# Three norm seams of a two-layer prefix model: the first tile's split, and when four weight splits are made

## The chip, the cores and the metric

The kernel runs on one NeuronCore of a Trainium2 chip. The metric is the device time of one execution in microseconds (us). Five engines have a part: TensorE (PE, with its weight loads as PEld), VectorE (DVE), ScalarE (ACT), GpSimd (POOL), and SyncE (SP), which issues the DMAs. They run side by side and wait for each other on semaphores.

## The reference, cut to what matters

Two layers work on 256 tokens of `x` and 256 of `ctx`. Each layer is a mixer (HGRN2 in layer 0, Mamba2 in layer 1) and a convolutional feed-forward net (FFN). Around each of these stands the same pattern:

```python
x = x + mx[2] * rmsnorm(yx, post_norm[l, 0])            # gate, norm and add what the mixer gave
hx = modulate(rmsnorm(x, pre_norm[l, 1]), mx[3], mx[4]) # norm again: h * (1 + scale) + shift
yx = conv_ffn(hx, ffn_w_up[l], ffn_w_down[l], ...)      # the next products read hx
```

All is float32. `rmsnorm` needs the mean square over all 1024 channels of a token.

## The kernel before, in words

Activations lie with channels on partitions: 8 tiles (KT = 8) of 128 channels x 512 tokens (256 where only `x` is left, in layer 1 from the mixer's end on). TensorE multiplies them in a split form: every operand is a rounded high part plus a low part, and a product is three matmuls, high*high, high*low, low*high. For activations these parts are `hh` and `hl`, for weights `wh` and `wl`. A weight block of 1024 columns per partition (8 k-tiles of 128x128) lands by DMA in one of four slots of `wraw`; ScalarE writes its high part (`split_hi`), VectorE (`split_lo`), or GpSimd in a loop of the FFN, its low part. VectorE's splits are counted by one semaphore, `w_lo_dve`, in the order of the blocks.

The order of each engine's work is written out by hand. Three times between two stages there is a *seam*, where `add_and_norm(l, s, n, weights)` runs on VectorE: seam 0 ahead of the first FFN (n = 512), seam 1 ahead of the Mamba projections (n = 512), seam 2 ahead of the second FFN (n = 256). Ahead of it VectorE makes `products` of each of the 8 output tiles (with ScalarE's squares), TensorE adds them up over the channels with a matrix of ones (`both_sums`), ScalarE makes a reciprocal root, and `variance` gives the second norm's mean square from the sums. TensorE then does one or two blocks of the modulation product (`ada_block`).

In `add_and_norm` VectorE runs over the tiles m: it "turns" tile m (`turn`: `sq <- yT * bank`, the first norm), adds it to `xT` (two instructions for the two halves of 256 tokens), turns tile m+1, and writes the second norm `tmp <- xT * bank`. ScalarE's `shift_high` scales and shifts `tmp` in place (two instructions) and copies it, rounded, to `hh`. GpSimd's `norm_low` writes `hl = tmp - hh`. After tile 0 VectorE does the splits of the blocks named in `weights`.

TensorE goes on with `by_tile`: a batch of three or four projections, k-tile by k-tile, so that it can start as soon as the first tile is there. Ahead of the batch it waits by `need_sub` for the last of the batch's weight blocks (in the FFN of both layers the fourth one, `u0 + 3`; at seam 1 block `("b", 0)`), and then for `hl_ready` of tile 0:

```python
need_sub(u0 + 2)
need_sub(u0 + 3)
by_tile(hl_count - KT, [up(0, 0), up(0, 1), up(1, 0), up(1, 1)], n)
```

Of the kernel before, what the change touches and what calls it, by code (L numbers as in the profile page):

```python
# [12 lines left out]
F32 = mybir.dt.float32  # L13
F32R = mybir.dt.float32r
U32 = mybir.dt.uint32
ALU = mybir.AluOpType
ACT = mybir.ActivationFunctionType
# [123 lines left out]
def program(nc, a, out):  # L141
# [542 lines left out]
    def _(pool):  # L684
# [81 lines left out]
        def norm_low(i, n):  # L766

            hh0 = (2, 3, 5)[i] * KT
            for k in range(KT):
                pool.wait_ge(hh_ready, hh0 + k + 1)  # L770
                pool.tensor_tensor(hl[:, k, 0:n], tmp[:, k % 2, 0:n], hh[:, k, 0:n].bitcast(F32), ALU.subtract).then_inc(hl_ready, 1)  # L771

# [37 lines left out]
    def _(act):  # L810
# [52 lines left out]
        def shift_high(i, l, s, n=T):  # L863

            for m in range(KT):
                if m < KT - 1:
                    hf[0] += 1
                    act.wait_ge(hf_ready, hf[0])
                else:
                    plan.wait_emptied(act, ("r2", i // 2, i % 2))  # L870
                t = tmp[:, m % 2, :]
                for b in range(n // SEQ):
                    r = slice(b * SEQ, (b + 1) * SEQ)
                    ins = act.activation(t[:, r], t[:, r], ACT.Identity, scale=nsc[:, l, s, m, b:b + 1],
                                         bias=mod[:, l, 3 * s * KT + m, b:b + 1])
                step(ins)
                step.wait()
                act.activation(hh[:, m, 0:n], t[:, 0:n], ACT.Copy).then_inc(hh_ready, 1)  # L878
# [451 lines left out]
    def _(dve):  # L1330
# [3 lines left out]
        def split_lo(n, i=0, lo=0, hi=None):  # L1334

            size = subs[n][0]
            hi = size if hi is None else hi
            if lo == 0:
                dve.wait_ge(w_hi, i * 4 + (n + 1))
            s = n % SLOTS  # L1340
            ins = dve.tensor_tensor(wl[:, s, lo:hi], wraw[:, s, lo:hi], wh[:, s, lo:hi].bitcast(F32), ALU.subtract)  # L1341
            if hi == size:
                ins.then_inc(w_lo["dve"], 1)
# [87 lines left out]
        def add_and_norm(l, s, n, weights):  # L1431

            i = 2 * l + s
            first, second = ("r", l, s), ("r2", l, s)
            turned = {}
            rn[0] += 1

            def turn(m):

                ins = V.tensor_tensor(sq[:, m % 2, 0:n], yT[:, m, 0:n], bank[plan.bank(first)][:, 0:n], ALU.mult)  # L1440
                if m < KT - 1:
                    turned[m] = step(ins)
                else:
                    plan.empty(ins, "dve", first)

            dve.wait_ge(rb_ready, i + 1)
            turn(0)
            for m in range(KT):
                if m < KT - 1:
                    step.wait(turned[m])  # L1450
                else:
                    plan.wait_emptied(dve, first)
                for b in range(n // SEQ):
                    r = slice(b * SEQ, (b + 1) * SEQ)
                    ins = V.scalar_tensor_tensor(out=xT[:, m, r], in0=sq[:, m % 2, r], scalar=gsc[:, l, s, m, b:b + 1],
                                                 in1=xT[:, m, r], op0=ALU.mult, op1=ALU.add)
                ins.then_inc(x_new, 1)
                xn[0] += 1
                if m < KT - 1:
                    turn(m + 1)  # L1460
                if m == 0:
                    dve.wait_ge(rstd_ready, rn[0])
                if m >= 2:
                    dve.wait_ge(hl_ready, KT * (i + 1) + m - 1)
                dve.wait_ge(x_new, xn[0])
                if (l, s, m) == (0, 1, 0):
                    plan.wait_ready(dve, ("am", LATE + 6))
                ins = V.tensor_tensor(tmp[:, m % 2, 0:n], xT[:, m, 0:n], bank[plan.bank(second)][:, 0:n], ALU.mult)
                if m < KT - 1:
                    ins.then_inc(hf_ready, 1)  # L1470
                else:
                    plan.empty(ins, "dve", second)
                if m == 0:
                    for w in weights:
                        split_lo(w)
            hhn[0] += KT

        xn, rn, norms = [0], [0], [0]
# [266 lines left out]
        gate_scales(0, 1)  # L1745
        step.wait()
        u0 = at["up", 0, 0, 0, 0]
        for m, pieces in enumerate(((at["y", 0, 5],), (at["y", 0, 6],), (at["y", 0, 7],), (), (u0,), (u0 + 1,), (u0 + 2,), ())):
            plan.wait_emptied(dve, ("y", 0, m))
            products(0, 0, 0, m, T)  # L1750
            for w in pieces:
                split_lo(w)
            if m == 3:
                ada_add(LATE + 2)
        variance(0, 0, T)
        add_and_norm(0, 0, T, (u0 + 3,))

        def taps(l, n):

# [101 lines left out]
        psum_freed_dve = plan.freed["dve"]  # L1861
        ffn_dve(0, T, True)
        variance(0, 1, T)
        add_and_norm(0, 1, T, (at["b", 0] - 1, at["b", 0]))

        u, e, w = dtw[:, 0, :], dtw[:, 1, :], dtw[:, 2, :]

# [242 lines left out]
            if m == 4:  # L2110
                ada_add(LATE + 10)
        variance(1, 0, SEQ)
        add_and_norm(1, 0, SEQ, [at["up", 1, 0, 1, j] for j in range(2)])
        ffn_dve(1, SEQ, False)
        dve.wait_ge(rstd_ready, rn[0] + 1)
        plan.wait_emptied(dve, ("xr", 1, 1))
# [637 lines left out]
```

## Time and profile before

| | |
|---|---|
| median of three runs | 1396.06 us (1392.92, 1396.06, 1396.13) |
| the profiled execution | 1392.95 us, its span 1391.2 us |
| TensorE busy | 1325.3 us, 95% of the span |
| VectorE, ScalarE, GpSimd busy | 894.1, 648.1, 331.6 us |
| mean granted TensorE clock | 0.986 of full speed |
| seam 0, seam 1, seam 2 | around 431, 812 and 1176 us |

TensorE is busy nearly all the time, and 82% of the chain of work that ended last is its matmuls. What is left are single stretches in which it waits. The profiled execution lies 3.1 us below the median of the three runs.

### The profile page before, as it was taken

The page shows a single profiled execution, that of the slowest core. Times are in us where ns is not written, and L with a number is a line of the kernel's source. Part 1 is how long each engine was busy: PE and PEld are TensorE (multiplying, and loading weights), DVE is VectorE, ACT ScalarE, POOL GpSimd, SP SyncE. Part 2 cuts the span into 40 slices and gives each one's busy share as a digit, 9 for nine tenths or more (in the row PEclk, how much of TensorE's full clock was granted, in tenths as well). Part 3 has the DMA queues.
Part 4 walks back from the last instruction along what each step waited for, and adds up shares of the span by engine and source line. Part 5 has one row for each costly group of instructions (what it writes and reads, how often), then busy time and mean ns, then how long its engine had stood idle before and what let it go on. Part 6 is the DMA issues. An engine that isn't in the chain of part 4 may idle for free.

```text
span 1391.2 us, 21288 instructions
## 1 busy us (share of the span) xinstructions
PE 1325.3 (95%) x7893; PEld 1118.1 (80%) x7893; DVE 894.1 (64%) x1706; ACT 648.1 (47%) x1023; POOL 331.6 (24%) x227
## 2 busy tenths in 40 slices
PE   5999999999998999999999989999999988899997
PEld 2678888888675888888888757888888877899997
DVE  4567777677587644322455778777777857665573
ACT  4435445444346433223333266555555645654554
POOL 1000000000202654105551030211111301780961
PEclk9999999999999999999999999999999999999999
DMA  9643343335461632333324424433333465456743
GB/s 346 180 133 125 122 129 127 125 90 184 152 202 41 181 91 76 91 106 109 102 68 136 116 96 122 152 92 91 91 91 91 137 207 157 124 164 176 203 134 107
DMA packets 274788, 183.16 MB, mean 132 GB/s; under 512 B 6643, under 2 KB 249107, under 8 KB 274707
## 3 DMA queue, kind: packets, MB, share of 16 engines
q1 hardware_dynamic: 274162, 180.00, 42.8%
q10 hardware_dynamic: 544, 2.10, 0.4%
q8 instruction: 49, 0.80, 0.2%
q14 instruction: 33, 0.26, 0.1%
HBM read 181.03 MB, written 1.05 MB: 131 GB/s over the span
## 4 chain that ended last, share of the span: by engine, by line
PE 82%; DVE 10%; ACT 5%; issue 2%; DMA 1%; POOL 0%; DVEq 0%; ACTq 0%
PE bank L2135 20%; PE bank L2137 20%; PE bank L2136 20%; DVE wl L1341 3%; PE bank L2150 2%; PE bank L2151 2%; PE bank L2152 2%; ACT wh L820 1%; PE bank L2201 1%; PE bank L2250 1%; DVE conv L1800 1%; PE bank L2682 1%; PE bank L2709 1%; PE bank L2277 1%; PE bank L2696 1%
## 5 line engine op out<-in xcount | busy, mean ns | idle before, releaser
L2135 PE MATMUL bank<-hh,wh 128*128 128x512 f32 (+1 forms) x1298 | 460.6, 355 | 10.2 <-DVE wl L1341 4.5
L2137 PE MATMUL bank<-hh,wl 128*128 128x512 f32 (+1 forms) x1298 | 455.8, 351 | 0.0
L2136 PE MATMUL bank<-hl,wh 128*128 128x512 f32 (+1 forms) x1298 | 455.6, 351 | 0.0
L820 ACT ACTIVATE wh<-wraw 128x1024 fp32r<-128x1024 f32 (+2 forms) x265 | 256.4, 985 | 108.9 <-PE bank L2137 97.4
L1341 DVE TENSOR_TENSOR wl<-wraw,wh 128x1024 fp32r<-128x1024 f32 (+2 forms) x187 | 205.8, 1122 | 136.6 <-ACT wh L820 136.5
L2135 PEld LDWEIGHTS bank<-hh,wh 128*128 128x128 f32 x1298 | 247.1, 190 | 45.0 <-DVE wl L1341 7.0
L2137 PEld LDWEIGHTS bank<-hh,wl 128*128 128x128 f32 x1298 | 247.1, 190 | 32.5
L2136 PEld LDWEIGHTS bank<-hl,wh 128*128 128x128 f32 x1298 | 247.2, 190 | 30.4
L1800 DVE SCALAR_TENSOR_TENSOR conv<-bank,pv,conv 128x189 f32<-128x189 f32 (+3 forms) x396 | 173.1, 437 | 131.9 <-ACT conv L1093 103.6
L711 POOL TENSOR_TENSOR wl<-wraw,wh 128x1024 fp32r<-128x1024 f32 x78 | 187.0, 2406 | 175.0 <-ACT wh L820 174.6
L2135 PE MATMUL bank<-fh,wh 128*128 128x512 f32 (+1 forms) x352 | 120.0, 341 | 3.5 <-DVE wl L1341 3.1
L2136 PE MATMUL bank<-fl,wh 128*128 128x512 f32 (+1 forms) x352 | 119.0, 338 | 0.0
L2137 PE MATMUL bank<-fh,wl 128*128 128x512 f32 (+1 forms) x352 | 119.0, 338 | 0.0
L756 POOL TENSOR_TENSOR hl<-yT,hh 128x512 fp32r<-128x512 f32 x13 | 19.0, 1487 | 369.7 <-DVE gates L1697 357.7
L2135 PEld LDWEIGHTS bank<-fh,wh 128*128 128x128 f32 x352 | 66.2, 188 | 12.1 <-issue 1.7
L771 POOL TENSOR_TENSOR hl<-tmp,hh 128x512 fp32r<-128x512 f32 (+1 forms) x24 | 27.9, 1164 | 196.1 <-ACT hh L878 196.1
L2137 PEld LDWEIGHTS bank<-fh,wl 128*128 128x128 f32 x352 | 66.2, 188 | 8.0
L2136 PEld LDWEIGHTS bank<-fl,wh 128*128 128x128 f32 x352 | 66.2, 188 | 7.9
L797 POOL TENSOR_TENSOR wx<-xtok,wtk 128x512 f32<-128x512 f32 x16 | 16.9, 1056 | 221.9 <-ACT xtok L1226 162.1
L1093 ACT ACTIVATE conv<-bank,pv 128x512 f32<-128x512 f32 (+1 forms) x44 | 29.4, 667 | 72.8 <-PE bank L2137 72.8
L731 POOL TENSOR_TENSOR fl<-prod,fh 128x512 f32 (+3 forms) x44 | 49.9, 1134 | 55.1 <-ACT fh L1109 55.1
L2150 PE MATMUL bank<-hh,wh 128*128 128x512 f32 (+2 forms) x119 | 47.5, 400 | 15.7 <-POOL hl L771 15.3
(338 smaller groups left out, 1936.2 us busy)
## 6 DMA issues: line engine op xcount, KB each, us to landing
wraw<-in_ffn_w_up SPq DMA_DIRECT2D x88, 512.0 KB, 3.9
araw<-in_ada_w SPq DMA_DIRECT2D x40, 1024.0 KB, 7.2
wraw<-in_mb_w_in SPq DMA_DIRECT2D x48, 512.0 KB, 4.1
wraw<-in_hg_w_in SPq DMA_DIRECT2D x40, 512.0 KB, 3.8
wraw<-in_ffn_w_down SPq DMA_DIRECT2D x32, 512.0 KB, 3.8
wraw<-in_mb_w_out SPq DMA_DIRECT2D x16, 512.0 KB, 4.4
gates<-in_ada_w SPq DMA_DIRECT2D x5, 1024.0 KB, 9.3
wraw<-in_hg_w_out SPq DMA_DIRECT2D x8, 512.0 KB, 4.8
```

The costliest lines, as they stand in the source:

```text
L711: pool.tensor_tensor(wl[:, n % SLOTS, 0:size], wraw[:, n % SLOTS, 0:size], wh[:, n % SLOTS, 0:size].bitcast(F32), ALU.subtract).then_inc(w ...
L731: pool.tensor_tensor(fl[:, bass.ds(i * 2 + c, 1), 0:w], prod[:, c % 2, 0:w].unsqueeze(1), fh[:, bass.ds(i * 2 + c, 1), 0:w].bitcast(F32), ...
L771: pool.tensor_tensor(hl[:, k, 0:n], tmp[:, k % 2, 0:n], hh[:, k, 0:n].bitcast(F32), ALU.subtract).then_inc(hl_ready, 1)
L820: act.activation(wh[:, n % SLOTS, 0:size], wraw[:, n % SLOTS, 0:size], ACT.Copy).then_inc(w_hi, 1)
L1093: act.activation(conv[:, u, 0:n], bank[2 * u if src is None else src][:, 0:n], ACT.Identity, scale=pv[:, bass.ds(i * 2 + (cw + c), 1)], bi ...
L1341: ins = dve.tensor_tensor(wl[:, s, lo:hi], wraw[:, s, lo:hi], wh[:, s, lo:hi].bitcast(F32), ALU.subtract)
L1800: ins = V.scalar_tensor_tensor(out=o(conv[:, u, :]), in0=src(bank[up]), scalar=pv[:, bass.ds(i * 2 + (cw + row * FT + c), 1)], in1=o(conv[ ...
L2135: pe.matmul(dst, W, hi(k), start=(k == 0), stop=False, **skip)
L2136: pe.matmul(dst, W, lo(k), start=False, stop=False, **skip)
L2137: ins = pe.matmul(dst, L, hi(k), start=False, stop=(k == nk - 1), **skip)
L2150: pe.matmul(dst, W, hi(k), start=(k == 0), stop=False, skip_group_check=True)
L2151: pe.matmul(dst, W, lo(k), start=False, stop=False, skip_group_check=True)
```

## The change

The matrix work and its order on TensorE stay as they are. On the other engines:

- ScalarE writes the shifted tile 0 straight into `hh[:, 0]` (rounded on the way), without the step over `tmp` and the copy.
- VectorE makes tile 0's low part itself: it shifts `tmp` a second time into `rsq` and subtracts `hh`. GpSimd begins with tile 1.
- In `add_and_norm` the norm of tile 0 comes ahead of the turn of tile 1.
- Weight splits: at seam 0 the splits of `u0 + 1` and `u0 + 2` move from behind the products of tiles 5 and 6 to behind those of tile 7. The splits inside `add_and_norm` move: at seam 0 the one from behind tile 0 to behind tile 1, at seam 1 the two from behind tile 0 to behind tiles 1 and 2, at seam 2 the second from behind tile 0 to behind tile 1.

```diff
@@ norm_low (GpSimd)
-            for k in range(KT):
+            pool.wait_ge(hl_ready, KT * (i + 1) + 1)
+            for k in range(1, KT):
@@ shift_high (ScalarE)
-                    ins = act.activation(t[:, r], t[:, r], ACT.Identity, scale=nsc[:, l, s, m, b:b + 1],
-                                         bias=mod[:, l, 3 * s * KT + m, b:b + 1])
+                    ins = act.activation(hh[:, 0, r] if m == 0 else t[:, r], t[:, r], ACT.Identity,
+                                         scale=nsc[:, l, s, m, b:b + 1], bias=mod[:, l, 3 * s * KT + m, b:b + 1])
+                if m == 0:
+                    ins.then_inc(hh_ready, 1)
+                    continue
@@ add_and_norm (VectorE)
-                if m < KT - 1:
+                if 0 < m < KT - 1:
                     turn(m + 1)
...
                 if m == 0:
-                    for w in weights:
-                        split_lo(w)
+                    turn(1)
+                    dve.wait_ge(hf_ready, KT + (KT - 1) * i + 1)
+                    for b in range(n // SEQ):
+                        r = slice(b * SEQ, (b + 1) * SEQ)
+                        ins = V.tensor_scalar(rsq[:, r], tmp[:, 0, r], nsc[:, l1, s1, 0, b:b + 1],
+                                              mod[:, l1, 3 * s1 * KT, b:b + 1], ALU.mult, ALU.add)
+                    step(ins)
+                    dve.wait_ge(hh_ready, hhn[0] + 1)
+                    step.wait()
+                    V.tensor_tensor(hl[:, 0, 0:n], rsq[:, 0:n], hh[:, 0, 0:n].bitcast(F32), ALU.subtract).then_inc(hl_ready, 1)
+                if m < 3 and weights[m] is not None:
+                    split_lo(weights[m])
@@ seam 0
-        for m, pieces in enumerate(((at["y", 0, 5],), (at["y", 0, 6],), (at["y", 0, 7],), (), (u0,), (u0 + 1,), (u0 + 2,), ())):
+        for m, pieces in enumerate(((at["y", 0, 5],), (at["y", 0, 6],), (at["y", 0, 7],), (), (u0,), (), (), (u0 + 1, u0 + 2))):
...
-        add_and_norm(0, 0, T, (u0 + 3,))
+        add_and_norm(0, 0, T, (None, u0 + 3, None))
@@ seam 1
-        add_and_norm(0, 1, T, (at["b", 0] - 1, at["b", 0]))
+        add_and_norm(0, 1, T, (None, at["b", 0] - 1, at["b", 0]))
@@ seam 2
-        add_and_norm(1, 0, SEQ, [at["up", 1, 0, 1, j] for j in range(2)])
+        add_and_norm(1, 0, SEQ, [at["up", 1, 0, 1, j] for j in range(2)] + [None])
```

VectorE's order at the end of seam 0's products, before (`gates` holds the running sums, `sq` the squares, `wl <-wraw,wh` is a weight split):

```order
L1410 TENSOR_TENSOR sq<-sq 128x512
L1341 TENSOR_TENSOR wl<-wraw,wh 128x1024
L1384 SCALAR_TENSOR_TENSOR gates<-yT,gsc,xT 128x256 x2
L1399 SCALAR_TENSOR_TENSOR gates<-sq,gsq,gates 128x256 x2
L1406 TENSOR_TENSOR gates<-gates 128x512
L1410 TENSOR_TENSOR sq<-sq 128x512
L1341 TENSOR_TENSOR wl<-wraw,wh 128x1024
L1384 SCALAR_TENSOR_TENSOR gates<-yT,gsc,xT 128x256 x2
L1399 SCALAR_TENSOR_TENSOR gates<-sq,gsq,gates 128x256 x2
L1418 TENSOR_TENSOR sq<-bank,rstd 128x512
```

and now:

```order
L1414 TENSOR_TENSOR sq<-sq 128x512
L1388 SCALAR_TENSOR_TENSOR gates<-yT,gsc,xT 128x256 x2
L1403 SCALAR_TENSOR_TENSOR gates<-sq,gsq,gates 128x256 x2
L1410 TENSOR_TENSOR gates<-gates 128x512
L1414 TENSOR_TENSOR sq<-sq 128x512
L1388 SCALAR_TENSOR_TENSOR gates<-yT,gsc,xT 128x256 x2
L1403 SCALAR_TENSOR_TENSOR gates<-sq,gsq,gates 128x256 x2
L1345 TENSOR_TENSOR wl<-wraw,wh 128x1024 x2
L1422 TENSOR_TENSOR sq<-bank,rstd 128x512
```

Both splits now stand behind the last tile's products, directly ahead of the variance.

VectorE's order in `add_and_norm` of seam 1, before (`tmp<-xT,bank` is the second norm of a tile):

```order
L1440 TENSOR_TENSOR sq<-yT,bank 128x512
L1455 SCALAR_TENSOR_TENSOR xT<-sq,gsc,xT 128x256 x2
L1440 TENSOR_TENSOR sq<-yT,bank 128x512
L1468 TENSOR_TENSOR tmp<-xT,bank 128x512
L1341 TENSOR_TENSOR wl<-wraw,wh 128x1024 x2
L1455 SCALAR_TENSOR_TENSOR xT<-sq,gsc,xT 128x256 x2
L1440 TENSOR_TENSOR sq<-yT,bank 128x512
L1468 TENSOR_TENSOR tmp<-xT,bank 128x512
```

and now, from the norm of tile 0 to the second split:

```order
L1473 TENSOR_TENSOR tmp<-xT,bank 128x512
L1445 TENSOR_TENSOR sq<-yT,bank 128x512
L1483 TENSOR_SCALAR rsq<-tmp,nsc,mod 128x256 x2
L1488 TENSOR_TENSOR hl<-rsq,hh 128x512
L1460 SCALAR_TENSOR_TENSOR xT<-sq,gsc,xT 128x256 x2
L1445 TENSOR_TENSOR sq<-yT,bank 128x512
L1473 TENSOR_TENSOR tmp<-xT,bank 128x512
L1345 TENSOR_TENSOR wl<-wraw,wh 128x1024
L1460 SCALAR_TENSOR_TENSOR xT<-sq,gsc,xT 128x256 x2
L1445 TENSOR_TENSOR sq<-yT,bank 128x512
L1473 TENSOR_TENSOR tmp<-xT,bank 128x512
L1345 TENSOR_TENSOR wl<-wraw,wh 128x1024
```

The second split stood five instructions behind the first turn; it now ends this row of twelve, behind the norms of tiles 1 and 2. At seams 0 and 2 the last split stands where the first one stands here, behind the norm of tile 1.

TensorE's rows where the batch of seam 0 begins, with the semaphores that they wait for (in the changed kernel; before they are the same but for line numbers):

```order
L2216 MATMUL bank<-gates,scc 32x512 x3
L2216 MATMUL bank<-alate,scc 32x512 [waits a_landed2]
L2216 MATMUL bank<-alate,scc 32x512 x3
L2165 MATMUL bank<-hh,wh 128x512 [waits hl_ready,w_lo_dve]
L2166 MATMUL bank<-hl,wh 128x512
L2167 MATMUL bank<-hh,wl 128x512
```

The first matmul of the batch waits for two things, tile 0's low part and VectorE's weight splits; nothing moved here.

## Rows read from the trace of the kernel before

**Rows 1.** Who TensorE waited for, whole span: total us, times, longest us.
```profile
PE bank L2150 <- POOL hl L771: 15.3, 4, 5.2
PE bank L2135 <- DVE wl L1341: 7.5, 7, 1.6
```

**Rows 2.** The chain of waits at seam 0: start us, us, what.
```profile
426.91 0.46 issue
427.37 0.69 DVE tmp L1468
428.08 1.10 ACT tmp L874 x2
429.20 0.64 ACT hh L878
429.91 1.27 POOL hl L771
431.32 0.77 PE bank L2150
```

**Rows 3.** Timeline of seam 0, VectorE: start us, us, instruction, idle before it.
```profile
418.00 1.22 DVE L1341 TENSOR_TENSOR wl<-wraw,wh 128x1024 fp32r<-128x1024 f32 x1
...
422.01 0.69 DVE L1418 TENSOR_TENSOR sq<-bank,rstd 128x512 f32<-128x512 f32 x1 [1.21 <-PE bank L2447]
...
426.77 0.68 DVE L1440 TENSOR_TENSOR sq<-yT,bank 128x512 f32<-128x512 f32 x1
...
427.96 1.22 DVE L1341 TENSOR_TENSOR wl<-wraw,wh 128x1024 fp32r<-128x1024 f32 x1
429.10 0.87 DVE L1455 SCALAR_TENSOR_TENSOR xT<-sq,gsc,xT 128x256 f32<-128x256 f32 x2
429.89 0.68 DVE L1440 TENSOR_TENSOR sq<-yT,bank 128x512 f32<-128x512 f32 x1
430.49 0.68 DVE L1468 TENSOR_TENSOR tmp<-xT,bank 128x512 f32<-128x512 f32 x1
```

**Rows 4.** Timeline of seam 0, TensorE's first sum of the squares.
```profile
418.23 1.10 PE L2445 MATMUL bank<-sq,ones 128*128 128x512 f32 x2 [2.57 <-DVE sq L1410]
```

**Rows 5.** Timeline of the first norm, VectorE: the shift and the low part.
```profile
33.13 0.73 DVE L1496 TENSOR_SCALAR tmp<-tmp,nsc,mod 128x256 f32<-128x256 f32 x2
33.78 0.69 DVE L1502 TENSOR_TENSOR hl<-tmp,hh 128x512 fp32r<-128x512 f32 x1
```

**Rows 6.** Timeline of seam 1: VectorE, GpSimd, TensorE.
```profile
808.16 0.68 DVE L1468 TENSOR_TENSOR tmp<-xT,bank 128x512 f32<-128x512 f32 x1
808.76 2.35 DVE L1341 TENSOR_TENSOR wl<-wraw,wh 128x1024 fp32r<-128x1024 f32 x2
811.03 1.88 DVE L1455 SCALAR_TENSOR_TENSOR xT<-sq,gsc,xT 128x256 f32<-128x256 f32 x2
...
810.71 1.52 POOL L771 TENSOR_TENSOR hl<-tmp,hh 128x512 fp32r<-128x512 f32 x1 [62.99 <-ACT hh L878]
...
812.38 0.77 PE L2150 MATMUL bank<-hh,wh 128*128 128x512 f32 x1 [5.25 <-POOL hl L771]
...
817.32 0.50 PE L2150 MATMUL bank<-hh,wh 128*128 128x512 f32 x1 [0.36 <-POOL hl L771]
```

**Rows 7.** Timeline of seam 2: VectorE, TensorE.
```profile
1172.83 0.42 DVE L1468 TENSOR_TENSOR tmp<-xT,bank 128x256 f32<-128x256 f32 x1 [0.16 <-ACT bank L861]
...
1176.25 0.55 PE L2150 MATMUL bank<-hh,wh 128*128 128x256 f32 x1 [4.73 <-POOL hl L771]
...
1179.15 0.58 PE L2150 MATMUL bank<-hh,wh 128*128 128x256 f32 x1
```

**Rows 8.** Windows of 7 us from each batch's start: us, PE busy, PEclk, DMA.
```profile
431.32:438.32 7.00, 7.00 (x19) 0.60 0.17 50
812.38:819.38 7.00, 6.63 (x21) 0.76 0.41 122
1176.25:1183.25 7.00, 6.99 (x39) 0.66 0.45 131
```

More of the change, by code:

```diff
@@ L1433, in add_and_norm @@
             i = 2 * l + s
+            l1, s1 = (i + 1) // 2, (i + 1) % 2
             first, second = ("r", l, s), ("r2", l, s)
```

## The prediction

> **What bounds the kernel now.** I read the page first: TensorE is busy for 95% of the span, so time is won or lost only where it waits. Then the list of who TensorE waited for [rows 1]: the largest entry is the first product of a batch waiting for a low part from GpSimd, 15.3 us in 4 waits, the three long ones at the three seams (about 5 us each [rows 6, 7]). Then the chain of waits at seam 0 [rows 2]: VectorE's norm of tile 0, ScalarE's shift (1.10) and copy (0.64), GpSimd's subtraction (1.27), and TensorE starts at 431.32. Last the timelines around the seams [rows 3 to 7] and the granted clock behind each start [rows 8]. The reader is to see there that the chain is what ended last *before*, and that a second condition, VectorE's last weight split, was met only shortly ahead of it: at 429.18 against 431.2 at seam 0 (427.96 + 1.22 [rows 3]), and at 811.11 against 812.23 at seam 1 (808.76 + 2.35 and 810.71 + 1.52 [rows 6]). TensorE's order, shown with the change, has both waits on the batch's first matmul. The change shortens the chain and moves the last split to behind the norm of tile 1 or 2. So the question at each seam is when that split ends.
>
> **The steps on VectorE.** Where instructions follow without a wait, the next starts about 0.08 before the last one's recorded end. From start to start, for 512 columns: a turn 0.60, the two adds to `xT` 0.79, a norm 0.60, a split 1.14 [rows 3]; the two shifts 0.65 [rows 5]. The low part takes 0.69 and frees VectorE after about 0.62 [rows 5].
>
> **What is won ahead of the first norm.** *Norm before turn.* The norm of tile 0 stood at 427.37, behind a turn begun at 426.77; in the chain that is 0.46 of "issue" [rows 2, 3]. Without the turn the norm starts once the adds have landed, 0.44 earlier. At seam 2 it is not the turn but ScalarE that it waits for (0.16 idle, released by ScalarE [rows 7]): nothing there. *Two splits behind the last products* (seam 0 only). TensorE's first sum waits 2.57 us for VectorE's sum of squares of tile 6 [rows 4], and one split stands ahead of that, so the sums come 1.1 earlier. The two splits then run behind tile 7's products, which end 2.2 earlier than before; they end when the sums are there, so the variance starts at 420.9 in place of 422.01 [rows 3]. Won: 1.1. In bounds from nothing (the splits push the variance back) to 1.2 (its idle time).
>
> **From the first norm to the last split.** Counted from the start of tile 0's norm: the turn of tile 1 begins at +0.60, the shifts at +1.20, done at about +1.9. ScalarE's two halves take +0.71 to +1.81 [rows 2]; a write rounded on the way is not in the trace with these operands; the copy of the same width costs 0.64 against 1.10 for the two halves, so I leave the 1.10 and bound an extra by 0 to 0.2. The low part starts at +1.9 and is there at +2.6, where it was at 431.18 - 427.37 = +3.8 before: 1.2 won on this leg. But VectorE is busy with it. Adds at +2.55, turn +3.35, norm of tile 1 +3.95, split +4.55 to +5.77, and TensorE starts 0.05 later. At seam 1 the adds, turn and norm of tile 2 follow (5.69 + 0.79 + 0.60 + 0.60), and the last split runs from +7.68 to +8.9.
>
> **Seam 0.** The norm starts at 427.37 - 1.1 - 0.44 = 425.83. Low part there at 428.4, but the split ends at 431.6, and TensorE starts at 431.65 against 431.32: **+0.35**. All that was won ahead is used up by the split's new place.
>
> **Seam 1.** The norm starts at 808.16 - 0.44 = 807.72, the last split ends at 816.6, TensorE starts at 816.7 against 812.38 [rows 6]: +4.3. Before, it had a second wait of 0.36 at 817.32 for tile 1; now tile 1 is ready (norm at 811.67, plus the 3.8 of the old chain is 815.5), so -0.36. After the first k-tile TensorE sets the pace itself, so nothing of the lost start comes back. Two smaller terms. The granted clock: in the 7 us behind the start it is 0.60, 0.76 and 0.66 [rows 8]; full speed being 2.4 GHz and the lower level 1.2, that is 5.6, 3.4 and 4.8 us at the lower one, and half of each is lost: 2.8, 1.7, 2.4. Seam 1, the cheapest, would now follow 9.6 us of idle time in place of 5.25. I put it near the mean of all, +0.6, in bounds of -1.7 to +1.1; the other two I leave, each within 1 either way. GpSimd: adds that began beside its subtraction took 1.88 in place of 0.87 [rows 3, 6]. The last split now begins at 815.4 while GpSimd works on tile 1 (814.3 to 815.6): +0.2, in bounds of 0 to 1.0. In sum **+4.7**.
>
> The Trainium skill (TensorE: Matmul & The Clock Gate, "What's actually happening") says that how many matmuls run at the half clock after a pause changes from run to run. The trace agrees in that the three seams differ, 3.4 to 5.6 us, after pauses alike. By that rule the clock term has no sign, and the sum would be 5.8 in place of 6.4.
>
> **Seam 2.** 256 columns. The norm stays at 1172.83. ScalarE's single piece (about 0.6 after the norm's end) is done at 1173.9, and the low part at 1174.4. VectorE: split to 1175.4, adds, turn and norm of tile 1 (0.40, 0.34, 0.34, as the 0.42 of [rows 7] less the overlap), second split 1176.5 to 1177.7. TensorE starts at 1177.8 against 1176.25: +1.55; the second k-tile, which came 2.90 after the first where 12 products at the lower clock need about 2.6 to 2.7, no longer waits: -0.2. **+1.35**.
>
> **Nothing elsewhere.** GpSimd loses three subtractions and is idle for tens of us ahead of them [rows 6]. The loads that reuse the slots of the late splits start up to 5 us later, but their blocks are wanted only behind the batch, over 15 us on. The norms of tiles 2 to 7 come 0.4 later at seam 0, some 4 us later at seam 1; TensorE, at 12 products per tile, stays behind them.
>
> **Sum.** 0.35 + 4.7 + 1.35 = 6.4 us, so the profiled execution of 1392.95 would become 1399.35. That execution lies 3.1 under the median of the three runs, 1396.06; against the median it is **1402.4**, of which the uncertain places take -2.5 to +3.
>
> **The rivals.**
> *The chain alone sets the start (faster).* If the last split did not hold the batch, TensorE would start with the low part: at seam 0 at 428.55 (-2.8; tile 2 at 436.7 gives back 0.4), at seam 1 at 810.45, bounded by tile 1 at 815.5 in place of 817.26 (-1.8), at seam 2 some -0.7. Together -4.9: 1391.2. For it speaks that GpSimd's chain is the wait that the profile names at all three seams; against it, that the batch's first matmul also waits for `w_lo_dve` and that the split's place is known to the instruction. 6%.
> *The late start is bought back (no change).* Behind each batch TensorE waits for a split again, 7.5 us in 7 waits over the kernel [rows 1]. Would these shrink by their mean of 1.1 behind each of the three batches, 3.2 us would be left: 1399.3. Against it: these splits wait for a slot that the batch's own last tile frees, so they move with it. Together with a lucky clock at the seams, 16%.
> *The dearer case (slower).* The pause at seam 1 makes the lower clock last as long as at seam 0 and longer, and the two-input work of VectorE and GpSimd collide at the split and at the adds behind it: +1.1 + 1.0 + 1.0 on the forecast, 1405.5. 12%.
>
> The Trainium skill (GPSIMD Engine Reference, "1. Specifications") says that GpSimd shares its way into SBUF with VectorE, and that they hinder each other where VectorE has two SBUF inputs, as its splits have. The 1.88 against 0.87 agrees; by that rule the last split at seam 1 would wait for GpSimd's end and start at about 815.6, the 0.2 taken above.
>
> **How the numbers follow.** The forecast, +6.4, has 66%, with a range of its own of 1399 to 1405.5. A change under 0.3% (4.2 us) can't be told from none. Slower: nine tenths of the forecast's 66 and the 12, 71%. No change: the 16, the rest of the forecast, and a part of the first rival, 25%. Faster: 4%. The range that should hold 8 in 10: 1396.5 to 1406.5; it takes in most of the case that buys time back and leaves out the faster one.
>
> **What would show it right or wrong.** In the profile of the changed kernel the first product of the batch should be released by VectorE's split `wl` and no more by a low part, at all three seams, with 5.5 to 6.5 us of idle time at seams 0 and 2 and about 9.5 at seam 1. The low part of tile 0, now VectorE's, should be there some 3 us ahead of it at seam 0 and 6 at seam 1. The variance of seam 0 should start about 1.1 earlier. Wrong would be a start of the batch right behind the low part, a batch at seam 1 that ends less than 3 us later against its seam's first norm than before, or a total under 1398.

## The result, and the profile after

| | before | changed |
|---|---|---|
| median of six runs each, us | 1392.76 (1390.88 to 1396.13) | 1400.13 (1397.81 to 1400.79) |
| span of the profiled execution, us | 1391.2 | 1398.7 |
| mean granted TensorE clock | 0.986 | 0.982 |

The changed kernel takes 1.0048 times as long, with a 95% interval of 1.0036 to 1.0060: slower, by about what was forecast (1402.4 against 1396.06, 1.0046). The profiled executions differ by 7.5 us.

Whom TensorE waited for, changed kernel, whole span (total us, times, longest us); this answers to [rows 1].

```profile
PE bank L2165 <- DVE wl L1345: 22.6, 3, 9.7
PE bank L2150 <- DVE wl L1345: 7.6, 7, 1.6
```

The wait for GpSimd's low part is gone from this list; in its place the batch waits three times for a weight split (`wl`), and longer. VectorE at seam 0, changed kernel (start us, us, instruction, idle before it), against [rows 3]:

```profile
423.94 0.43 DVE L1433 TENSOR_SCALAR ssx<-ssx 128x512 f32<-128x512 f32 x1
...
425.98 0.69 DVE L1473 TENSOR_TENSOR tmp<-xT,bank 128x512 f32<-128x512 f32 x1
426.59 0.68 DVE L1445 TENSOR_TENSOR sq<-yT,bank 128x512 f32<-128x512 f32 x1
427.19 0.73 DVE L1483 TENSOR_SCALAR rsq<-tmp,nsc,mod 128x256 f32<-128x256 f32 x2
428.02 0.69 DVE L1488 TENSOR_TENSOR hl<-rsq,hh 128x512 fp32r<-128x512 f32 x1
428.63 0.88 DVE L1460 SCALAR_TENSOR_TENSOR xT<-sq,gsc,xT 128x256 f32<-128x256 f32 x2
429.42 0.68 DVE L1445 TENSOR_TENSOR sq<-yT,bank 128x512 f32<-128x512 f32 x1
430.02 0.68 DVE L1473 TENSOR_TENSOR tmp<-xT,bank 128x512 f32<-128x512 f32 x1
430.62 1.22 DVE L1345 TENSOR_TENSOR wl<-wraw,wh 128x1024 fp32r<-128x1024 f32 x1
```

The norm of tile 0 starts 1.39 earlier than before (425.98 for 427.37), and its low part is there at 428.71. TensorE starts only at 431.93, 0.09 behind the end of the split at 431.84. Seam 1, VectorE and GpSimd, against [rows 6]:

```profile
808.51 0.69 DVE L1473 TENSOR_TENSOR tmp<-xT,bank 128x512 f32<-128x512 f32 x1
...
810.54 0.69 DVE L1488 TENSOR_TENSOR hl<-rsq,hh 128x512 fp32r<-128x512 f32 x1
...
813.14 1.22 DVE L1345 TENSOR_TENSOR wl<-wraw,wh 128x1024 fp32r<-128x1024 f32 x1
...
816.26 1.24 DVE L1345 TENSOR_TENSOR wl<-wraw,wh 128x1024 fp32r<-128x1024 f32 x1
...
815.15 1.27 POOL L772 TENSOR_TENSOR hl<-tmp,hh 128x512 fp32r<-128x512 f32 x1 [66.68 <-ACT hh L882]
```

TensorE where the three batches start, changed kernel; the last row is the next wait behind the batch of seam 1:

```profile
431.93 0.76 PE L2165 MATMUL bank<-hh,wh 128*128 128x512 f32 x1 [6.58 <-DVE wl L1345]
817.56 0.80 PE L2165 MATMUL bank<-hh,wh 128*128 128x512 f32 x1 [9.66 <-DVE wl L1345]
1184.66 0.55 PE L2165 MATMUL bank<-hh,wh 128*128 128x256 f32 x1 [6.34 <-DVE wl L1345]
...
843.69 0.39 PE L2150 MATMUL bank<-hh,wh 128*128 128x256 f32 x1 [0.64 <-DVE wl L1345]
```

and that last row in the kernel before:

```profile
837.96 0.39 PE L2135 MATMUL bank<-hh,wh 128*128 128x256 f32 x1 [0.64 <-DVE wl L1341]
```

At seam 1 the low part of tile 0 is done at 811.23, 6.3 us ahead of its first use. No second wait is left in that batch. Windows of 7 us from each start (us, busy times, then PEclk, DMA share, GB/s), against [rows 8]:

```profile
431.93:438.93 7.00, 7.00 (x19) 5.53 (x20) 7.00 (x13) 4.05 (x8) 3.82 (x3) 0.58 0.27 77
817.56:824.56 7.00, 7.00 (x19) 5.07 (x20) 7.00 (x13) 4.03 (x8) 3.78 (x3) 0.57 0.28 76
1184.66:1191.66 7.00, 7.00 (x43) 7.00 (x44) 6.70 (x16) 4.69 (x10) 4.00 (x5) 0.71 0.40 115
```

At seam 1 the clock is 0.57 where it was 0.76: the cheap seam has become as dear as seam 0.

**Where the 7.5 us are.** How far the changed execution lags at each landmark: 0.1 ahead of seam 0, 0.8 ahead of seam 1 (seam 0 itself cost 0.7), 5.7 behind seam 1's batch (5.0), 6.8 ahead of seam 2 (1.1), 7.9 behind it (1.1), 7.5 at the end. The 1.1 between seams 1 and 2 is one wait, in the Mamba layer, at a place where no instruction was moved. VectorE there, first the kernel before, then the changed one with GpSimd and TensorE beside it:

```profile
1108.58 0.73 DVE L1969 COPY_PREDICATED wd<-past,wd 128x512 f32<-128x512 uint32 x1
```

```profile
1114.32 1.85 DVE L1984 COPY_PREDICATED wd<-past,wd 128x512 f32<-128x512 uint32 x1
1111.47 5.79 POOL L756 TENSOR_TENSOR hl<-yT,hh 128x512 fp32r<-128x512 f32 x4
1116.89 0.63 PE L2228 MATMUL bank<-ident,asum 128*128 128x128 f32 x4 [1.09 <-DVE wd L1976]
```

GpSimd in the kernel before, at the same moment:

```profile
1108.58 1.83 POOL L756 TENSOR_TENSOR hl<-yT,hh 128x512 fp32r<-128x512 f32 x1
```

In both traces a subtraction of GpSimd begins together with the copy. Before, the copy kept its 0.73 and the subtraction took 1.83; in the changed kernel the copy took 1.85, and the subtraction beside it 1.26. One of the two loses time to the other, and TensorE waits only where it is VectorE. In the profiles of all ten experiments below the copy lost (1.85 or 1.86) and the wait of 1.1 is there, and one of them (e5) has no instruction of the change, only matmuls of constants in the pauses. So no part of the change is needed for it; the profile of before is the one without it. What decides which of the two loses was not tried.

### The profile page after: what moved, and what is told of

Its sections match the earlier page's. It is cut to its first block, busy times and chain, and to the rows that moved or that the text cites. A ratio compares the mean times of both kernels' runs of the same rounds, so it can differ in the third digit from the quotient of the medians.

```text
span 1398.7 us, 21296 instructions
## 1 busy us (share of the span) xinstructions
PE 1326.2 (95%) x7893; PEld 1118.4 (80%) x7893; DVE 893.9 (64%) x1714; ACT 646.1 (46%) x1020; POOL 327.6 (23%) x224
## 3 DMA queue, kind: packets, MB, share of 16 engines
HBM read 181.03 MB, written 1.05 MB: 130 GB/s over the span
## 4 chain that ended last, share of the span: by engine, by line
PE 81%; DVE 11%; ACT 4%; issue 1%; DMA 1%; SPq 1%; POOL 0%; DVEq 0%; ACTq 0%
PE bank L2150 20%; PE bank L2152 20%; PE bank L2151 20%; DVE wl L1345 3%; PE bank L2165 2%; PE bank L2216 2%; PE bank L2166 2%; PE bank L2167 2%; DMA gates<-in_ada_w 1%; ACT wh L821 1%; PE bank L2265 1%; DVE conv L1815 1%; PE bank L2724 1%; PE bank L2292 1%; PE bank L2711 1%
## 5 line engine op out<-in xcount | busy, mean ns | idle before, releaser
L772 POOL TENSOR_TENSOR hl<-tmp,hh 128x512 fp32r<-128x512 f32 (+1 forms) x21 | 23.6, 1123 | 199.9 <-ACT hh L882 199.9
```

## The experiments

Each kernel was run against the kernel before on the same chip. For the seams one measure is used throughout: the time from the start of `variance`'s last instruction on VectorE (`ssx`, 423.94 above) to the first row behind the batch in which TensorE waits (843.69 above). "Start" is the time to the batch's first matmul. The ratios rest on 5 to 12 runs of each kernel, the two columns on the right on one profiled execution each.

| kernel | ratio to before (95%) | start, seams 0 / 1 / 2 | to the batch's end, seams 0 / 1 / 2 |
|---|---|---|---|
| before | 1 | 6.4 / 6.7 / 5.0 | 31.5 / 32.3 / 20.5 |
| changed | 1.0048 (1.0036, 1.0060) | 8.0 / 11.1 / 6.7 | 33.2 / 37.2 / 21.6 |
| e1 own block | 1.0005 (0.9995, 1.0015) | 4.8 / 5.0 / 3.3 | 30.2 / 34.0 / 21.4 |
| e2 splits back | 1.0004 (0.9995, 1.0013) | 6.0 / 7.1 / 5.6 | 31.3 / 33.2 / 20.9 |
| e3 only splits | 1.0034 (1.0021, 1.0047) | 7.5 / 11.5 / 5.5 | 32.6 / 37.3 / 20.8 |
| e4 changed, pauses filled | 1.0007 (0.9998, 1.0016) | 8.0 / 11.1 / 6.7 | 30.5 / 34.5 / 20.0 |
| e5 before, pauses filled | 0.9988 (0.9978, 0.9998) | 6.4 / 6.7 / 5.1 | 29.3 / 33.8 / 19.7 |
| e7 own block, filled | 1.0008 (0.9999, 1.0017) | 4.8 / 5.0 / 3.3 | 31.4 / 34.0 / 20.9 |
| e8 own block, early supply | 0.9983 (0.9974, 0.9992) | 4.8 / 5.0 / 3.3 | 31.3 / 32.1 / 20.6 |
| e6 e8, filled | 0.9983 (0.9974, 0.9992) | 4.8 / 5.0 / 3.3 | 31.3 / 32.1 / 20.8 |
| e9 before, one split early, filled | 0.9953 (0.9939, 0.9967) | 6.4 / 6.4 / 5.1 | 29.3 / 30.1 / 19.7 |
| e10 e9, norms first, filled | 0.9969 (0.9955, 0.9983) | 6.1 / 6.1 / 5.3 | 30.0 / 30.8 / 19.8 |

**e1: each product waits for its own block.** The changed kernel, with the wait for the batch's last block replaced by one wait per product at its first k-tile.

```diff
-                    need_sub(u0 + 2)
-                    need_sub(u0 + 3)
-                    by_tile(hl_count - KT, [up(0, 0), up(0, 1), up(1, 0), up(1, 1)], n)
+                    by_tile(hl_count - KT, [up(0, 0), up(0, 1), up(1, 0), up(1, 1)], n, own=[u0 + j for j in range(4)])
@@ by_tile; likewise at seam 1
-                for dst, w, nk, finish in products:
+                for j, (dst, w, nk, finish) in enumerate(products):
+                    if own is not None and k == 0:
+                        need_sub(own[j])
```

> The changed kernel; only TensorE's waits differ: each product of the batch waits for its own weight block at the first k-tile, where all four used to be waited for ahead of the first matmul. Theory A (the last split holds the batch's start): the batch starts with VectorE's low part of tile 0, about 3.1 us earlier than in the changed kernel at seam 0 (428.8), 6.1 at seam 1 (811.4) and 3.3 at seam 2. The last block is wanted only after nine matmuls, so seam 0 no longer waits for it, seams 1 and 2 wait a little inside the first k-tile. The end of the batches moves by -2.9, -4.2 and -1.8 us (less what the clock takes): about -9 against the changed kernel, -1.5 to -2.5 against the one before (1390 to 1391). Theory B (VectorE's added work on tile 0 is what costs, the splits do not): no gain beyond 1 us, 1399 to 1400.

Median 1394.04; the span is 7.7 shorter than the changed kernel's. TensorE's waits in the batches of this kernel, seams 0 to 2:

```profile
PE bank L2167 <- DVE hl L1488: 10.0, 3, 3.6
PE bank L2167 <- DVE wl L1345: 4.0, 4, 1.8
PE bank L2167 <- POOL hl L772: 0.4, 1, 0.4
```

The starts are now released by VectorE's low part (`hl`) and come 3.2, 6.1 and 3.4 sooner. So the split's gate on the first matmul is what the change paid for. But the batch only reaches the splits later: at seam 1 it waits 0.46 and 1.76 for them, and ends 1.7 later than before. Starting early on the low part wins at seam 0 alone. That is less than expected (1390 to 1391): against the changed kernel the batches end 3.1, 3.2 and 0.2 sooner, where I had 2.9, 4.2 and 1.8.

**e2: the splits of `add_and_norm` back.** The changed kernel, with both splits right behind tile 0's low part.

```diff
-                if m < 3 and weights[m] is not None:
-                    split_lo(weights[m])
+                if m == 0:
+                    for w in weights:
+                        if w is not None:
+                            split_lo(w)
```

> The changed kernel with the splits of add_and_norm back behind tile 0, now right behind its low part; the two splits behind the last products stay. Theory A: the last split ends about +3.85 us behind the norm of tile 0 at seam 0 (it was +5.85), +5.0 at seam 1 (+9.0) and +3.85 at seam 2 (+5.0). TensorE starts 2.0, 4.0 and 1.1 us earlier than in the changed kernel: -7.1 in sum, 1393, no difference from before that can be measured. Theory B: VectorE's added work is still there, so no more than 1 us is won against the changed kernel.

Median 1393.8, as expected: the loss is gone although VectorE still makes tile 0's low part. The split still releases all three starts, after 4.6, 5.7 and 5.3 us.

**e3: only the splits move.** The kernel before with the splits at their new places (two at seam 0 ahead of the variance, four inside `add_and_norm`) and nothing else.

```diff
                 if m == 0:
-                    for w in weights:
-                        split_lo(w)
+                if m < 3 and weights[m] is not None:
+                    split_lo(weights[m])
@@ seam 0, 1, 2
+        pieces (), (), (u0 + 1, u0 + 2) behind tiles 5, 6, 7
+        weights (None, u0 + 3, None); (None, at["b", 0] - 1, at["b", 0]); [..., None]
```

> The kernel before with only the moves of the splits (two behind the last products at seam 0; behind tiles 1 and 2 in place of tile 0). Low part of tile 0 by GpSimd as before. Theory A: the last split ends +3.75 us behind the norm of tile 0 at seam 0, level with the low part, so only the 1.1 of the products is won; at seam 1 the split ends at about 815.1, TensorE starts +2.8 against before; at seam 2 +0.35. With 0.7 of clock at seam 1: +2.5 against before, 1395.3. The rest of the change's +7 (some 4.5) is then what VectorE's new work in front of the split costs. Theory B: the moves alone cost nothing, 1391 to 1392.

Measured +5.0 us (1398.18 for 1393.17), twice what I expected. VectorE, GpSimd and TensorE at seam 1 of this kernel:

```profile
811.96 2.89 DVE L1455 SCALAR_TENSOR_TENSOR xT<-sq,gsc,xT 128x256 f32<-128x256 f32 x2
...
810.78 3.78 POOL L771 TENSOR_TENSOR hl<-tmp,hh 128x512 fp32r<-128x512 f32 x2 [63.00 <-ACT hh L878]
...
817.23 0.80 PE L2149 MATMUL bank<-hh,wh 128*128 128x512 f32 x1 [10.03 <-DVE wl L1341]
```

GpSimd's subtractions of tiles 0 and 1 now lie beside the first split (810.82 to 812.04) and the adds of tile 2. The split keeps its 1.22 and the subtraction beside it takes 2.38; the adds take 2.89 in place of 0.87, and the two subtractions together 3.78 in place of 2 x 1.27. The last split moves back by those 2 us as well. At seam 0 it is the slowed subtraction itself that the batch waits for (7.5 for 6.4). So the moved splits alone cost 5 of the 7.4 us. With the low part on VectorE too, the batches end 0.6 later, 0.1 sooner and 0.8 later, and the intervals of the two kernels overlap. That it costs so little fits the traces, in which the changed kernel has no subtraction of tile 0 on GpSimd to collide with; this was not tried apart. The two halves don't add up, and my division of the loss between them was wrong.

**e4: the pauses filled, changed kernel.** TensorE multiplies constants (24, 36 and 24 matmuls of 128x128 into a bank that is overwritten later) in the three pauses. They leave the supply as it is and keep the engine at work.

```diff
+        def keep_busy(count):
+            for _ in range(count):
+                pe.matmul(bank[3][:, 0:P], ones[:, :], ident[:, :], start=True, stop=True)
@@ ahead of each of the three batches
+        keep_busy(24)      # 36 at seam 1, 24 at seam 2
```

> The changed kernel; TensorE fills the pause of each seam with small matmuls of constants into a bank that is overwritten later (24, 36 and 24 of 128x128, some 5.2, 7.8 and 5.2 us), and waits then as before. If the low clock behind each batch's start (5.9, 6.0 and 4.1 us of the first 7 in the changed kernel) comes from the pause and not from the batch itself, the granted clock stays at 1.0 and half of that time is won back: 2.9 + 3.0 + 2.0 = -8 against the changed kernel, 1392. If the clock falls all the same, no difference; if the fill delays the batch, the start is released by nothing on VectorE and comes later than 431.9.

Median 1393.75, 6.4 under the changed kernel where I had expected 8. The fill at seam 1 (36 matmuls, each recorded as two), the batch's start behind it, and the window from there:

```profile
805.16 8.30 PE L2174 MATMUL bank<-ident,ones 128*128 128x128 f32 x72
814.90 0.50 PE L2165 MATMUL bank<-hh,wh 128*128 128x512 f32 x1 [1.44 <-DVE wl L1345]
```

```profile
814.90:821.90 7.00, 7.00 (x31) 5.27 (x32) 7.00 (x13) 4.01 (x7) 3.80 (x3) 1.00 0.29 78
```

The batches start as late as in the changed kernel (same "start" column) and run at full clock: they end 2.8, 2.7 and 1.6 sooner. That is the price of the lower clock at the seams, measured apart from the waiting: 7.1 us in all, where the windows above give 2.9, 3.0 and 2.0 (half of the time at the lower level). The median spans agree with it, 1391.4 for 1398.4. The times gain less because in six of e4's eleven executions the time lies 2.4 to 3.5 over the span, where it is 1.7 to 1.9 in every other kernel; why is open.

**e5: the pauses filled, kernel before** (19, 20 and 18 of the same matmuls).

> The kernel before; TensorE fills the three pauses (5.0, 5.25 and 4.7 us) with 19, 20 and 18 small matmuls of constants, about 0.23 us each by the last runs. Theory C (the low clock behind a seam is paid only where TensorE, not the supply of tiles, sets the pace): seam 0 wins until tile 1 holds it, -1.9; seam 1 nothing, since its second k-tile already waited for tile 1 and ran at full clock from there; seam 2 -0.9. Sum -2.8 against before. Theory D (every us at the low clock costs half a us): 2.8 + 1.7 + 2.4 = -6.9.

Median 1391.29: only 1.5 us won where the three seams could have given 6.9 by [rows 8] (2.8, 1.7 and 2.4) and the other of my two recorded sums was 2.8. Seams 0 and 2 ended 2.2 and 0.8 sooner. Seam 1 got worse, 33.8 in place of 32.3, in a profiled execution (1393.75) that lies 2.5 above the median. The second wait in its batch, and the window behind it:

```profile
815.33 0.50 PE L2150 MATMUL bank<-hh,wh 128*128 128x512 f32 x1 [1.90 <-POOL hl L771]
```

```profile
817.43:824.43 7.00, 7.00 (x28) 5.30 (x27) 7.00 (x13) 5.13 (x10) 2.96 (x3) 0.86 0.01 2
```

At full clock the first k-tile is used up sooner, tile 1 isn't there, the wait grows from 0.36 [rows 6] to 1.90, and behind it the clock falls after all. Not every such wait has this sequel: at seam 2 of the same profile the batch waits 1.23 for tile 1, and the 7 us behind it ran at 1.00.

**e7: own block and fill together** (e1 with 12, 12 and 10 matmuls), **e8: own block with an earlier supply** (e1, and `norm` of tile 1 ahead of turn 2, the first of seam 1's two splits ahead of `variance`), **e6: e8 with e7's fill.** The edit of e8 over e1:

```diff
-                if 0 < m < KT - 1:
+                if 1 < m < KT - 1:
                     turn(m + 1)
...
+                if m == 1:
+                    turn(2)
                 if m < 3 and weights[m] is not None:
@@ seam 1 (and its split_hi ahead of the rsqrt)
+        split_lo(at["b", 0] - 1)
         variance(0, 1, T)
-        add_and_norm(0, 1, T, (None, at["b", 0] - 1, at["b", 0]))
+        add_and_norm(0, 1, T, (None, at["b", 0], None))
```

> The changed kernel with each product of the batch waiting for its own block, the fills (12, 12, 10 small matmuls), the norm of tile 1 ahead of the turn of tile 2, and at seam 1 block b0-1 split ahead of the variance, where VectorE waited 1.96 us (ScalarE makes its high part ahead of the root), block b0 behind tile 1. If tile 1's low part is what holds the batch once its start is free and the clock is up, the time from the variance to the end of the batch falls from 31.5 to 29.6 us at seam 0, from 32.3 to 30.8 at seam 1, from 20.5 to about 19.5 at seam 2, and 1.0 is won ahead of seam 0: -5.4 against before, 1387.5. If a split ahead of the variance pushes ScalarE's root back, seam 1 wins nothing: 1389.

> The changed kernel with each product waiting for its own block, and the fills, nothing else. Against the same without fills (1391.0 in its profile, its clock low again inside the batches of seams 1 and 2): seam 0 -0.2 (tile 1 holds it), seam 1 -1.6, seam 2 -1.8: 1387.5 in the profile. If waits of 1.8 and 1.6 us inside the batch lower the clock by themselves, nothing is won at seams 1 and 2: 1391.

> The version e6 without the fills. Against own blocks alone: seam 0 -0.5 (tile 1 earlier), seam 1 -2 (b0 is split 2.3 us earlier, so the wait inside the first k-tile and the second low clock go), seam 2 -0.3: about 1388.5 in the profile. If the low clock holds TensorE so long that the earlier tile 1 is not used, seam 0 wins nothing.

e7 missed its expectation of 1387.5: 1394.35, no better than e1. Its batch at seam 1:

```profile
812.65 0.50 PE L2167 MATMUL bank<-hh,wh 128*128 128x512 f32 x1 [1.30 <-DVE wl L1345]
815.80 0.50 PE L2167 MATMUL bank<-hh,wh 128*128 128x512 f32 x1 [2.18 <-DVE wl L1345]
```

Windows of 7 us from a wait in each of its three batches (at seam 0 from the first of two, 0.76 and 1.10 us long):

```profile
432.00:439.00 7.00, 5.90 (x18) 4.38 (x19) 7.00 (x13) 4.05 (x8) 3.81 (x3) 0.76 0.26 75
815.80:822.80 7.00, 7.00 (x24) 5.09 (x25) 7.00 (x13) 4.03 (x8) 3.79 (x3) 0.76 0.28 76
1180.30:1187.30 7.00, 6.59 (x40) 6.38 (x41) 6.71 (x16) 4.66 (x9) 3.99 (x5) 0.76 0.39 115
```

The waits moved into the batch, and in all three batches the lower clock came back (0.76). e6 and e8 measured 1391.11 and 1390.86, alike, and both missed: I had expected 1387.5 of e6 and 1388.5 of e8's profiled execution, which took 1391.07. The fill was worth nothing there. Both wait for tile 2 inside a batch, 1.59 at seam 0 in e8 and 1.57 at seam 1 in e6. Windows of 7 us behind these waits at seams 0 and 1 of e6:

```profile
438.48:445.48 7.00, 7.00 (x31) 5.80 (x32) 7.00 (x13) 4.14 (x8) 3.89 (x3) 1.00 0.00 0
819.03:826.03 7.00, 7.00 (x31) 5.26 (x32) 7.00 (x13) 4.15 (x8) 3.88 (x3) 1.00 0.00 0
```

Here the clock stayed up behind waits as long as some of e7's, while behind one of 1.69 at seam 2 of e6 it fell to 0.76. What decides it these runs don't show. In e6, VectorE at seam 0 and GpSimd beside it:

```profile
432.20 1.90 DVE L1460 SCALAR_TENSOR_TENSOR xT<-sq,gsc,xT 128x256 f32<-128x256 f32 x2
...
432.48 1.33 POOL L772 TENSOR_TENSOR hl<-tmp,hh 128x512 fp32r<-128x512 f32 x1 [61.65 <-ACT hh L882]
```

The norm drawn ahead of the turn puts GpSimd's subtraction beside the adds, which lose 1.0. Once the batch begins early, the tiles' supply is the bound at seams 0 and 1: behind its start at seam 1 e8 ran at 0.56 and e6 at 1.00, and both end after 32.1; a start 1.6 sooner than in the kernel before ends the batch 0.2 sooner.

**e9: the kernel before, with one split early and the pauses filled.** It keeps GpSimd's low part and the split behind tile 0. Seam 0's two splits go behind the last products (as in the change), the first of seam 1's two splits ahead of `variance`, and the fill is e5's.

```diff
@@ seam 1 (and its split_hi ahead of the rsqrt)
+        split_lo(at["b", 0] - 1)
         variance(0, 1, T)
-        add_and_norm(0, 1, T, (at["b", 0] - 1, at["b", 0]))
+        add_and_norm(0, 1, T, (at["b", 0],))
```

> The kernel before with the pauses filled (19, 20, 18 small matmuls), the two splits of seam 0 behind the last products, and at seam 1 block b0-1 split ahead of the variance; GpSimd makes all low parts, one split behind tile 0 at seams 0 and 1. Theory (tile 1 and the clock together hold the batch): with fills alone seam 1 had a wait of 1.9 us for tile 1 and a low clock of 3.4 us inside the batch behind it. One split less ahead of tile 1 brings it 1.1 us earlier, the wait falls to about 0.8, and no low clock follows: variance to end of batch 33.8 -> 31.1. Seam 0 29.3 as with fills alone, and begins 1.0 earlier; seam 2 19.7. Sum -5 against before: 1387.5 to 1388. Rival (the clock falls from any wait in the batch): seam 1 stays at 32.5 or more.

Median 1387.07, ratio 0.9953: 5.9 us under the kernel before, better than either kernel. (Its profiled execution, 1389.11, is the slowest of its five.) VectorE at seam 1, and TensorE's start:

```profile
797.80 1.23 DVE L1341 TENSOR_TENSOR wl<-wraw,wh 128x1024 fp32r<-128x1024 f32 x1
799.82 0.69 DVE L1418 TENSOR_TENSOR sq<-bank,rstd 128x512 f32<-128x512 f32 x1 [0.80 <-PE bank L2453]
...
809.15 0.47 PE L2151 MATMUL bank<-hh,wh 128*128 128x512 f32 x1 [0.34 <-POOL hl L771]
```

The early split stands in time in which VectorE waits for TensorE's sums anyhow: 0.80 of it is still left. Tile 1 now comes 1.1 sooner behind tile 0, and that batch has no wait inside. Seam 1 went from 33.8 (e5) to 30.1, where I had expected 31.1. The other move, of seam 0's two splits, lets `variance` begin 1.0 sooner than in e5; the two were not run apart.

**e10: e9 with the norms of tiles 0 and 1 ahead of the next turn.** The fill is two matmuls shorter at seams 0 and 1 (17, 18 and 18).

```diff
-                if m < KT - 1:
+                if 1 < m < KT - 1:
                     turn(m + 1)
...
+                if m < 2:
+                    turn(m + 1)
                 if m == 0:
```

> As e9, and the norms of tiles 0 and 1 ahead of the turns of tiles 1 and 2 at all seams. If nothing else moved, tile 0 would be 0.44 and tile 1 0.5 us earlier: -1 more over seams 0 and 1. Rival, from the version with own blocks and early splits: VectorE's adds of tile 2 then begin beside GpSimd's subtraction and take 1.9 in place of 0.9 us, so tile 2 comes later, and nothing is won or up to 1 us lost per seam.

Median 1389.13, 2 us worse than e9; the two intervals overlap, but the profiles agree, with batches that end 0.7 later at seams 0 and 1. The starts come 0.3 sooner there, but the batches then wait 1.08 and 1.05 for tile 1, where e9 had no wait. (Behind both waits the clock stayed at 1.00.) VectorE's adds of tile 1 and GpSimd's subtraction of tile 0:

```profile
428.36 1.88 DVE L1455 SCALAR_TENSOR_TENSOR xT<-sq,gsc,xT 128x256 f32<-128x256 f32 x2
...
428.58 1.39 POOL L771 TENSOR_TENSOR hl<-tmp,hh 128x512 fp32r<-128x512 f32 x1 [57.99 <-ACT hh L878]
```

So the turn ahead of the norm is no loss with one split behind tile 0, as in e9 and at seam 0 of the kernel before: there GpSimd's first subtraction falls beside a turn and a norm, and the adds keep their 0.87.

## Why the prediction was right

**The gate.** Right, and shown: e1 takes the split off the first matmul, e2 puts the splits back, and either brings the ratio to 1.0005 or 1.0004. The rival that the chain alone sets the start is out. Counted from tile 0's norm at seam 1, I had the low part there after 2.6 (measured 2.7), the last split from 7.68 to 8.9 (7.75 to 8.99), the start after it 0.1 later (0.06).

**The absolute number.** The time measured, 1400.13, lies 2.3 under the 1402.4 of the forecast, and that closeness is in part luck: the base, the median of three runs, was 3.3 above the median of six (1392.76), and the rise, 6.4, was 1.0 short of the 7.4 between the medians. In the profiled executions the rise is 7.5.

**Ahead of the first norm, seam 0.** Forecast 1.54 earlier (1.1 by the late splits, 0.44 by the order); it came 1.39 earlier in an execution that lagged by 0.10, so 1.49. ScalarE's rounded write took 1.09 for the two halves; my bound of 0 to 0.2 extra was not needed.

**Seam 0, +0.35: measured +0.7.** The start is 0.5 late and not 0.35, by small steps (0.83 from the shifts' start to the low part's, where I had 0.7), and the low clock lasts a little longer, 0.58 for 0.60.

**Seam 1, +4.7: measured +5.0.** The start is 4.4 late (forecast 4.3). *The clock is the mis-sized term*: between matmul starts of 0.43 and of 0.23 us one counts 14 slow ones behind the start where there were 8, 6 x 0.20 = 1.2 us in place of the 0.6 that I took near the mean. That is just outside my upper bound of +1.1. The vanished second wait was worth more than its 0.36: the matmul starts around it lay 0.76 apart in place of 0.23, so 0.5. The collision term (+0.2) was not needed: the split took 1.24. The Trainium skill (GPSIMD Engine Reference, "1. Specifications") has contention wherever VectorE reads two SBUF inputs. The two overlapped here by only 0.16 (816.26 to 816.42), so this row doesn't weigh it. e3's rows agree with it, but there it was the subtraction that took longer (2.38 for 1.27) while the split beside it kept 1.22, and not the split, as I had taken it. Terms by the trace: 4.4 - 0.5 + 1.2 = 5.1.

**Seam 2, +1.35: measured +1.1.** The start is 1.6 late; the clock window is 0.71 for 0.66, which gives 0.35 back. The Trainium skill (TensorE: Matmul & The Clock Gate, "What's actually happening") says that the number of matmuls at the lower clock varies between runs of one kernel. The seams moved by +0.1, +1.2 and -0.35 us, in both directions, and the mean clock of the kernel before lay between 0.984 and 0.990 over 35 runs, which agrees. How much of seam 1's 1.2 comes from the longer pause stays open: each kernel has one profile. The length of the pause alone doesn't set it: ahead of seam 1 TensorE idled 3.59 in both e1 and e8, and the next 7 us ran at 0.76 in one and at 0.56 in the other.

**The late start is not bought back**, as forecast: behind each batch the next wait is unchanged (0.43, 0.64 and 1.39 in both kernels).

**What I had not seen.** The collision between GpSimd's subtraction and VectorE's adds took 2 us at seam 1 of e3 and what the order of e10 should have won; I weighed it only as a tail risk, and it was in the rows (1.88 and 1.52 [rows 6]). Ahead of the changed kernel's batches no adds are slowed (0.88, 0.87), which I had not worked out: that is luck. And the sum of seams explains 6.8 us; another 1.1 in the profiles is the wait of the Mamba layer that belongs to no part of the change.

## What to carry to other kernels

Before shortening the chain that a wait names, list every semaphore of the waiting instruction and when each is met: the second one here was met only 2.0 us (seam 0) and 1.1 us (seam 1) ahead of the one that the profile names, and the change pushed exactly that one back. Work that must be done before a batch starts belongs where its engine is idle for another engine's sake (ahead of the variance), not between the first tiles' steps. And two faults of a pause, starting late and running slow afterwards, can be priced apart by filling it with matmuls of constants; but the fill pays only if the supply keeps up. Otherwise the wait moves into the batch, and in e5 and e7 the lower clock came back behind it.

## What the runs showed of the hardware

- Fills of 128x128 float32 matmuls (0.23 us each: 8.30 us for 36) kept the granted clock at 1.00 through pauses of 5 to 10 us, but for the last 0.3 to 1.4 us, and behind them (e4, e9). A wait of 1.90 us inside the batch behind such a fill was followed by the lower clock (0.86 in a window of 7 us, e5); so were the waits of 1.1 to 2.2 in e7 (0.76) and one of 1.69 in e6 (0.76). Other waits of 1.0 to 1.6 were not (1.00 behind 1.23 in e5, 1.57 and 1.59 in e6, 1.03 to 1.08 in e10).
- VectorE's pair of adds (0.87) took 1.9 where it lay fully beside one GpSimd subtraction and 2.9 beside two; the subtraction took 1.3 to 1.6 for 1.27, and the two 3.78. This happens behind the starts too, at every second tile of either kernel (1.93 at 433.07 before, 1.92 at 435.73 changed). A weight split kept its 1.22 and the subtraction beside it took 2.38 (e3). A predicated copy and a subtraction that began together took 0.73 and 1.83 in one profile, 1.85 and 1.26 in eleven others: one kept its time, the other took longer, by a little less than the first one lasts. VectorE's turns and norms, with one input in PSUM, kept their 0.68 beside GpSimd.
